# The transposed block's read, queued in front of a weight load instead of behind it

## The chip, the cores and the metric

The kernel runs on one core of a Trainium2 chip. The metric is device time in microseconds (us), median of three runs. One execution was also profiled: each instruction's start and duration, each DMA's issue and landing, and the clock granted to TensorE, which is full speed over the whole span.

## What the reference computes

A trunk of two layers over x of 256 positions by 2048 features. Each layer is a mixer (retention and a gated recurrence in layer 0, block attention in layer 1), an output projection, and then the part that matters here, a gated MLP with a causal convolution of width 3:

```python
def conv_ffn(h, w_up, conv_w, conv_b, w_down):
    u = causal_dwconv(h @ w_up, conv_w, conv_b)
    gate, val = jnp.split(u, 2, axis=-1)
    return (jax.nn.gelu(gate) * val) @ w_down
```

`w_up` is 2048 by 11264 (gate and value halves of 5632), `w_down` is 5632 by 2048, in float32.

## The kernel before

**Chunks and the ring.** All weights are streamed from DRAM in chunks of 256 rows by 512 columns (512 KB), 784 of them. A ring of four slots (`RING`) holds them. SyncE (SP) issues each load into `raw` (`load`, L322) once VectorE (DVE) has finished with the chunk four earlier in the same slot (`lo_ready`). ScalarE (ACT) rounds the chunk to `w_hi` (L498), DVE subtracts to get the rest, `w_lo` (L1147), and TensorE (PE) multiplies with both, 12 matmuls per chunk in up (L892 to L894). ACT may start a chunk only when it has landed and PE has used the chunk four earlier.

**A block of up.** Up has 22 blocks of 512 columns per layer: for each of 11 pairs a gate block (half 0) and a value block (half 1). A block is 8 chunks (c = 0 to 7). Pair 0 is written out, pairs 1 to 10 are a hardware loop over j, and down follows. PE writes a block with positions on the partitions, while the convolution wants features on them. So while the next block's chunks stream, the block is turned:

- after its `w_lo` of chunk 2, DVE transposes the block in 32 by 32 squares from PSUM to `cross` (L1310, L1311) and signals `acc_drained`;
- SP writes `cross` to the DRAM tensor `turn_line` with four DMAs of 128 KB (`put`, L342), behind the load of chunk 6 in its order;
- SP waits for the four to land (`put_out`), reads `turn_line` back to `h` with one DMA of 512 KB (`fetch`, L359), and signals `moved`;
- after `w_lo` of chunk 7, DVE scales `h` by the row norms (L1317), which waits for `moved`;
- ACT, after its `w_hi` of the following chunk 0, applies the first tap (L564, four instructions), which waits for L1317;
- DVE applies the two other taps after `w_lo` of chunks 1 and 2 (L1324, L1331), then transposes the next block, and so on.

Every engine goes through its instructions in program order; the order of SP is the order in which its transfers are queued. The loads that stand around a `fetch` are called A (chunk 7), B (chunk 0 of the next block) and C (chunk 1) below. ACT has a table load before `w_hi` of chunk 0 in every loop iteration (L498 ACT_TABLE_LOAD); so half of the Bs, those that open an iteration, have it behind them. A gate block is turned during the value block's chunks, so its `fetch` stands beside such a B; for a value block B is chunk 0 of half 1, and has no table load.

Of the kernel before, what the change touches and what calls it, by code (L numbers as in the profile page):

```python
# [130 lines left out]
def build(nc, x_t, params, w_gates, rope, decay, rel_bias, buckets, identity,  # L131
# [180 lines left out]
    @block.sync  # L312
    def _(sp):
        def load(w, q, c, cols, rows):

            s = c % RING
            turn = q + c // RING
            if not (isinstance(turn, int) and turn == 0):

                sp.wait_ge(lo_ready, RING * (turn - 1) + s + 1)  # L320
            src = w[bass.ds(rows * (CT * P), CT * P), cols].rearrange("(t p) n -> p t n", p=P)
            sp.dma_start(raw[:, s, :, :], src).then_inc(landed[s], 16)  # L322

        def put(n):

            sp.wait_ge(acc_drained, n + 1)
            write_quads()

        def put_x(k):

            sp.wait_ge(x_flipped, k + 1)
            write_quads()

        def put_qk(k):

            sp.wait_ge(qk_flipped, k + 1)
            write_quads()

        def write_quads():
            for i in range(QUADS):  # L340
                dst = turn_line[:, i, :].rearrange("(g c) n -> c g n", g=QUADS)
                sp.dma_start(dst, flip_quads[i * SQ:(i + 1) * SQ, :, :]).then_inc(put_out, 16)  # L342

        def put_probs(i):

            sp.wait_ge(probs_flipped, i + 1)
            for k in range(QUADS):
                dst = prob_line[:, k, :].rearrange("(g c) n -> c g n", g=QUADS)
                sp.dma_start(dst, probs_flip[k * SQ:(k + 1) * SQ, :, :]).then_inc(probs_out, 16)

        def fetch_probs(i):

            sp.wait_ge(probs_out, 16 * QUADS * (i + 1))
            sp.dma_start(probs_back[:, :, :], prob_line[:, :, :]).then_inc(probs_moved, 16)

        def fetch(k):

            sp.wait_ge(put_out, 16 * QUADS * (k + 1))
            sp.dma_start(h_quads[:, :, :], turn_line[:, :, :]).then_inc(moved, 16)  # L359

        for ph in phases:
            l = ph.layer
            for b, (_, _, col) in enumerate(ODD_BLOCKS if l else EVEN_BLOCKS):
                for c in range(KC):
                    if (l, b, c) == (0, 0, 0):
                        for u, landing in enumerate((tile_landed, landed[0])):
                            sp.dma_start(raw[:, 0, u, :], w_in[0][u * P:(u + 1) * P, col:col + NB]).then_inc(landing, 16)
                        continue
                    if (l, b, c) == (0, 0, 5):
                        sp.dma_start(par[:, 4 * KT:], params[:, 4 * KT:]).then_inc(const_loaded, 16)  # L370
                    load(w_in[l], ph.q_in + 2 * b, c, slice(col, col + NB), c)
                    if l and b >= 2 and b % 3 != 1 and b < 3 * MOVED_QK + 1:
                        k = 2 * ((b - 2) // 3) + (b % 3 == 0)
                        if c == 2:
                            put_qk(k)
                        if c == 4:
                            fetch(ph.m_in + k)
                    if l == 0 and b - 2 in MOVED_IN and c == 0:
                        fetch(MOVED_IN.index(b - 2))
                    if l == 0 and b - 1 in MOVED_IN and c == 6:  # L380
                        put(b - 1)
                    if l and b in (4, 7, 10) and c == 7:
                        put_probs(b // 3 - 1)
                    if l and b in (5, 8, 11) and c == 1:
                        fetch_probs(b // 3 - 1)
                    if (l, b, c) == (0, 0, 1):

                        sp.wait_ge(tile_landed, 16)
                    if (l, b) == (0, 0) and c in (1, 3, 4):
                        j = (1, 3, 4).index(c) + 1  # L390
                        part = slice(j * BT, (j + 1) * BT)
                        sp.dma_start(x_res[:, part, :], x_t[:, part, :]).then_inc(x_loaded[j], 16)
            for b in range(OUTB):
                for c in range(KC):
                    load(w_out[l], ph.q_out + 2 * b, c, slice(b * NB, (b + 1) * NB), MIX_ORDER[l][c])
                    if b >= 2 and c == 0:
                        fetch(ph.m_out + b - 2)
                    if b and c == 6:
                        put(ph.n_out + b - 1)
            for half in range(2):  # L400
                for c in range(KC):
                    load(w_up[l], ph.q_up + 2 * half, c, slice(half * D_FF, half * D_FF + NB), c)
                    if half == 0 and c == 0:
                        fetch(ph.m_up - 1)
                    if half and c == 6:
                        put(ph.n_up)
            with sp.Fori(1, PAIRS) as j:
                for half in range(2):
                    for c in range(KC):
                        load(w_up[l], ph.q_up + 4 * j + 2 * half, c, bass.ds(j * NB + half * D_FF, NB), c)  # L410
                        if c == 0:
                            fetch(ph.m_up + 2 * j + half - 2)
                        if c == 6:
                            put(ph.n_up + 2 * j + half - 1)
            for b in range(OUTB):
                cols = slice(b * NB, (b + 1) * NB)
                for c in range(FC) if b == 0 else DOWN_HEAD:
                    load(w_down[l], ph.q_down, FC * b + c, cols, c)
                    if b == 0 and c in (0, 8):
                        fetch(ph.m_down - 2 + c // 8)  # L420
                    if b == 0 and c == 6:
                        put(ph.n_down - 1)
                    if l and (b, c) == (0, 18):
                        put_x(0)
                    if l and (b, c) == (0, 20):
                        fetch(ph.m_down)
                    if l and b and c == 7:
                        put_x(b)
                    if l and b and c == 9:
                        fetch(ph.m_down + b)  # L430
                    if b and l == 0 and c == 6:
                        put(ph.n_down + b - 1)
                    if b and l == 0 and c == 8:
                        fetch(ph.m_down + b - 1)
                if b == 0:
                    continue
                with sp.Fori(*DOWN_TURNS) as t:
                    for i in range(RING):
                        load(w_down[l], ph.q_down + t, FC * b + i, cols, RING * t + i)
                for c in DOWN_TAIL:  # L440
                    load(w_down[l], ph.q_down, FC * b + c, cols, c)

        for t in range(2):

            sp.wait_ge(last_added, t + 1)
            sp.dma_start(out_t[:, t, (OUTB - 1) * NB:], x_nat[:, OUTB - 1, t, :]).then_inc(last_stored, 16)
        sp.wait_ge(last_stored, 16 * 2)
# [1367 lines left out]
```

## Time and profile before

| | us |
|---|---|
| median of three runs | 2202.23 |
| lowest, highest | 2201.97, 2204.25 |
| the profiled execution | 2206.41 |
| its span, first to last instruction | 2204.6 |
| PE busy, in the span | 2194.8 |
| DVE busy | 1514.0 |
| ACT busy | 1151.9 |
| share of the 16 DMA engines taken by SP's queue | 70.9% |

Up of layer 0 lies at about 360 to 870 us of the span, up of layer 1 at about 1460 to 1970. Ends of matmuls are modelled and overlap the next one's start, so gaps of PE are read from starts.

### The profile page before, as it was taken

What the parts mean: (1) busy time and instruction counts of PE and PEld (TensorE: products, weight loads), DVE (VectorE), ACT (ScalarE), POOL (GpSimd) and SP (SyncE); (2) the same over time, 40 slices, a digit from 0 to 9 for tenths busy, and PEclk for the clock granted to TensorE, in tenths of its full rate; (3) what the DMA queues carried; (4) which work ended last, traced back from release to release, by engine and by line L of the source; (5) the groups of instructions that cost most, each with busy time, mean ns of one, the idle gap of its engine ahead of it and who ended that gap; (6) DMA issues with size and microseconds to landing.
All of it is one profiled execution on the core that took longest, in us unless ns stands there. A gap on an engine that the chain in (4) does not pass through costs nothing.

```text
span 2204.6 us, 28872 instructions
## 1 busy us (share of the span) xinstructions
PE 2194.8 (100%) x10010; PEld 1827.4 (83%) x10010; DVE 1514.0 (69%) x1927; ACT 1151.9 (52%) x1440; POOL 7.7 (0%) x17
## 2 busy tenths in 40 slices
PE   9999999999999999999999999999999999999999
PEld 8888888888888888888888888888887888888887
DVE  7877766777777776655566576676777677766444
ACT  6554455555655655444455555555555556554443
POOL 0000000000000000000000000000000000000000
PEclk9999999999999999999999999999999999999999
DMA  8766667777787877766676786567777878777665
GB/s 272 216 214 202 203 207 224 224 236 242 236 250 233 249 229 248 222 203 206 205 232 216 223 265 200 182 217 239 231 238 227 249 234 248 230 248 240 216 214 162
DMA packets 267938, 497.97 MB, mean 226 GB/s; under 512 B 18790, under 2 KB 55670, under 8 KB 267729
## 3 DMA queue, kind: packets, MB, share of 16 engines
q1 hardware_dynamic: 265968, 490.68, 70.9%
q0 software_dynamic: 1456, 5.65, 0.7%
q8 instruction: 51, 0.84, 0.1%
q10 hardware_dynamic: 432, 0.56, 0.1%
q14 instruction: 31, 0.25, 0.0%
HBM read 456.16 MB, written 40.66 MB: 225 GB/s over the span
## 4 chain that ended last, share of the span: by engine, by line
PE 75%; DVE 8%; DMA 8%; issue 4%; ACT 3%; SPq 1%; DVEq 1%; ACTq 0%
PE ps L892 13%; PE ps L894 13%; PE ps L893 13%; PE ps L874 8%; PE ps L875 8%; PE ps L876 8%; DMA h<-turn_line 6%; PE ps L851 5%; PE ps L855 3%; ACT w_hi L498 1%; DMA turn_line<-cross 1%; DVE w_lo L1147 1%; DVE h L1317 1%; DVE pad_g L1331 1%; DVE pad_g L1324 1%
## 5 line engine op out<-in xcount | busy, mean ns | idle before, releaser
L1147 DVE TENSOR_TENSOR w_lo<-raw,w_hi 128x1024 fp32r<-128x1024 f32 x782 | 947.0, 1223 | 560.8 <-ACT w_hi L498 535.2
L498 ACT ACTIVATE w_hi<-raw 128x1024 fp32r<-128x1024 f32 x782 | 812.6, 1056 | 687.0 <-PE ps L876 256.3
L892 PE MATMUL ps<-w_hi,xs 128*128 128x512 f32 x2048 | 800.1, 391 | 2.1 <-DVE w_lo L1147 2.1
L893 PE MATMUL ps<-w_lo,xs 128*128 128x512 f32 x2048 | 797.6, 389 | 0.0
L894 PE MATMUL ps<-w_hi,xs 128*128 128x512 f32 x2048 | 797.6, 389 | 0.0
L892 PEld LDWEIGHTS ps<-w_hi,xs 128*128 128x128 f32 x2048 | 384.6, 188 | 84.0 <-DVE w_lo L1147 4.8
L894 PEld LDWEIGHTS ps<-w_hi,xs 128*128 128x128 f32 x2048 | 384.6, 188 | 80.1
L893 PEld LDWEIGHTS ps<-w_lo,xs 128*128 128x128 f32 x2048 | 384.6, 188 | 78.8
L874 PE MATMUL ps<-w_hi,act 128*128 128x512 f32 x808 | 315.0, 390 | 1.0 <-DVE w_lo L1147 1.0
L876 PE MATMUL ps<-w_hi,act 128*128 128x512 f32 x808 | 314.6, 389 | 0.0
L875 PE MATMUL ps<-w_lo,act 128*128 128x512 f32 x808 | 314.6, 389 | 0.0
L874 PEld LDWEIGHTS ps<-w_hi,act 128*128 128x128 f32 x808 | 151.7, 188 | 33.3 <-DVE w_lo L1147 1.4
L876 PEld LDWEIGHTS ps<-w_hi,act 128*128 128x128 f32 x808 | 151.7, 188 | 31.4
L875 PEld LDWEIGHTS ps<-w_lo,act 128*128 128x128 f32 x808 | 151.8, 188 | 31.2
L851 PE MATMUL ps<-act,w_hi 128*128 128x512 f32 (+1 forms) x304 | 95.5, 396 | 0.0
L1317 DVE TENSOR_TENSOR h<-h,rstd 128x1024 f32<-128x1024 f32 x44 | 53.9, 1226 | 43.6 <-DMA h<-turn_line 43.1
L851 PE MATMUL ps<-xs,w_hi 128*128 128x512 f32 x256 | 81.0, 398 | 2.0 <-DVE w_lo L1147 1.5
L855 PEld LDWEIGHTS ps<-act,w_lo 128*128 128x128 f32 x304 | 57.2, 188 | 13.4
L572 ACT ACTIVATE act<-pad_v 128x1024 f32 (+1 forms) x22 | 23.4, 1064 | 81.1 <-DVE pad_v L1341 81.1
L564 ACT ACTIVATE pad_v<-h,par 128x256 f32<-128x256 f32 x88 | 45.8, 592 | 34.4 <-DVE h L1317 34.4
L855 PE MATMUL ps<-act,w_lo 128*128 128x256 f32 (+1 forms) x304 | 59.8, 278 | 0.0
L855 PEld LDWEIGHTS ps<-xs,w_lo 128*128 128x128 f32 x256 | 48.1, 188 | 11.2
(209 smaller groups left out, 1132.6 us busy)
## 6 DMA issues: line engine op xcount, KB each, us to landing
raw<-w_up SPq DMA_DIRECT2D x352, 512.0 KB, 4.6
raw<-w_in SPq DMA_DIRECT2D x191, 512.0 KB, 4.4
raw<-w_down SPq DMA_DIRECT2D x176, 512.0 KB, 4.7
turn_line<-cross SPq DMA_DIRECT2D x276, 128.0 KB, 2.5
h<-turn_line SPq DMA_DIRECT2D x69, 512.0 KB, 6.0
raw<-w_out SPq DMA_DIRECT2D x64, 512.0 KB, 4.7
prob_line<-probs_t SPq DMA_DIRECT2D x12, 192.0 KB, 3.7
probs<-prob_line SPq DMA_DIRECT2D x3, 768.0 KB, 6.2
```

Of the source, the lines that this page charges most:

```text
L498: act_f(w_hi[:, s, :, :], raw[:, s, :, :], ACT.Copy).then_inc(hi_ready, 1)
L564: ins = act_f(by_quad(pad[:, t, 0:S]), h_tiles[:, :, t, :], ACT.Identity, scale=w, bias=b)
L851: return mm(ps[:, 4 * group + m, :], w_hi[:, s, u, m * P:(m + 1) * P], rhs, start=first and u == 0, stop=False)
L855: return mm(ps[:, 4 * group + m, 0:S], w_lo[:, s, u, m * P:(m + 1) * P], rhs[:, 0:S], start=False, stop=last and u == CT - 1)
L874: mm(out, x_hi, w_hi[:, s, u, :], start=first and u == 0, stop=False)
L875: mm(out, x_hi, w_lo[:, s, u, :], start=False, stop=False)
L876: ins = mm(out, x_lo, w_hi[:, s, u, :], start=False, stop=last and u == CT - 1)
L892: mm(out, x_hi, w_hi[:, s, u, :], start=first and u == 0, stop=False)
L893: mm(out, x_hi, w_lo[:, s, u, :], start=False, stop=False)
L894: ins = mm(out, x_lo, w_hi[:, s, u, :], start=False, stop=last and u == CT - 1)
L1147: tt(w_lo[:, s, :, :], raw[:, s, :, :], w_hi[:, s, :, :].bitcast(F32), ALU.subtract).then_inc(lo_ready, 1)
L1317: tt(h_tiles, h_tiles, scale, ALU.mult).then_inc(normed, 1)
```

## The change

In the whole of up, and in the first 9 chunks of down, `fetch` is issued one load earlier in SP's order: directly behind A instead of directly behind B. The number of transfers, their sizes, their targets and what each waits for stay the same. The read of the out projection's last block (`fetch(ph.m_up - 1)`) stays where it is.

```diff
                     if half and c == 6:
                         put(ph.n_up)
+                    if half and c == 7:
+                        fetch(ph.m_up)
             with sp.Fori(1, PAIRS) as j:
                 for half in range(2):
                     for c in range(KC):
                         load(w_up[l], ph.q_up + 4 * j + 2 * half, c, bass.ds(j * NB + half * D_FF, NB), c)
-                        if c == 0:
-                            fetch(ph.m_up + 2 * j + half - 2)
                         if c == 6:
                             put(ph.n_up + 2 * j + half - 1)
+                        if c == 7:
+                            fetch(ph.m_up + 2 * j + half - 1)
             for b in range(OUTB):
                 cols = slice(b * NB, (b + 1) * NB)
                 for c in range(FC) if b == 0 else DOWN_HEAD:
                     load(w_down[l], ph.q_down, FC * b + c, cols, c)
-                    if b == 0 and c in (0, 8):
-                        fetch(ph.m_down - 2 + c // 8)
+                    if b == 0 and c == 7:
+                        fetch(ph.m_down - 1)
```

## Rows read from the trace of the kernel before

**Rows 1.** Waits of PE over the whole span: total us, times, longest.
```profile
PE ps L892 <- DVE w_lo L1147: 2.1, 5, 0.9
PE ps L874 <- DVE w_lo L1147: 1.0, 1, 1.0
```

**Rows 2.** Timeline of PE at the last gap: start, us, [idle before <- releaser].
```profile
1968.51 0.39 PE L876 MATMUL ps<-w_hi,act 128*128 128x512 f32 x1
1969.91 0.50 PE L874 MATMUL ps<-w_hi,act 128*128 128x512 f32 x1 [1.01 <-DVE w_lo L1147]
```

**Rows 3.** Waits view of DVE for the read-back block, whole span.
```profile
DVE h L1317 <- DMA h<-turn_line: 43.1, 40, 2.9
```

**Rows 4.** Chain that ended last, layer 1: first and last L1317 of 21.
```profile
1515.57 1.24 DVE h L1317
...
1957.39 1.24 DVE h L1317
```

**Rows 5.** Timeline of SP, a gate block's turn: issues.
```profile
1814.03 1.79 SPq L342 DMA_DIRECT2D turn_line<-cross  x4
1818.02 0.40 SPq L322 DMA_DIRECT2D raw<-w_up  x1
1818.57 0.36 SPq L359 DMA_DIRECT2D h<-turn_line  x1
```

**Rows 6.** The same for the value block's turn just before it.
```profile
1792.47 1.79 SPq L342 DMA_DIRECT2D turn_line<-cross  x4
1795.20 0.40 SPq L322 DMA_DIRECT2D raw<-w_up  x1
1796.47 0.35 SPq L359 DMA_DIRECT2D h<-turn_line  x1
```

**Rows 7.** Waits of SP's queue for the four writes, whole span.
```profile
SPq L359 <- DMA turn_line<-cross: 47.5, 45, 2.9
```

**Rows 8.** Load B of rows 5, by its line: issue to landing.
```profile
DMA to landing us min/median/max: 5.0/5.0/5.0
```

**Rows 9.** Chain, pieces of the two reads: issue, us until landing.
```profile
1796.47 6.06 DMA h<-turn_line
...
1818.57 5.94 DMA h<-turn_line
```

**Rows 10.** Timeline of ACT behind the two Bs, value block first.
```profile
1801.39 1.06 ACT L498 ACTIVATE w_hi<-raw 128x1024 fp32r<-128x1024 f32 x1 [0.28 <-DMA raw<-w_up]
1803.96 2.08 ACT L564 ACTIVATE pad_v<-h,par 128x256 f32<-128x256 f32 x4 [1.51 <-DVE h L1317]
...
1823.08 1.28 ACT L498 ACT_TABLE_LOAD   x1 [2.05 <-DMA raw<-w_up]
1824.37 1.06 ACT L498 ACTIVATE w_hi<-raw 128x1024 fp32r<-128x1024 f32 x1
1826.01 2.08 ACT L564 ACTIVATE pad_g<-h,par 128x256 f32<-128x256 f32 x4 [0.57 <-DVE h L1317]
1828.00 3.02 ACT L498 ACTIVATE w_hi<-raw 128x1024 fp32r<-128x1024 f32 x3
```

**Rows 11.** Timeline of DVE: L1317 of three blocks (value, value, gate).
```profile
1715.78 1.23 DVE L1317 TENSOR_TENSOR h<-h,rstd 128x1024 f32<-128x1024 f32 x1 [1.56 <-DMA h<-turn_line]
...
1802.55 1.23 DVE L1317 TENSOR_TENSOR h<-h,rstd 128x1024 f32<-128x1024 f32 x1 [0.18 <-DMA h<-turn_line]
...
1824.53 1.23 DVE L1317 TENSOR_TENSOR h<-h,rstd 128x1024 f32<-128x1024 f32 x1 [1.03 <-DMA h<-turn_line]
```

**Rows 12.** Timeline of SP, the first read of layer 0 and load C.
```profile
415.01 0.35 SPq L359 DMA_DIRECT2D h<-turn_line  x1
415.65 0.39 SPq L322 DMA_DIRECT2D raw<-w_up  x1
```

**Rows 13.** Timeline of DVE, the first L1317 of layer 0.
```profile
419.76 1.23 DVE L1317 TENSOR_TENSOR h<-h,rstd 128x1024 f32<-128x1024 f32 x1 [0.60 <-DMA h<-turn_line]
```

**Rows 14.** Timeline of DVE and PE, fourth chunk of down in layer 0.
```profile
867.66 1.23 DVE L1147 TENSOR_TENSOR w_lo<-raw,w_hi 128x1024 fp32r<-128x1024 f32 x1
...
869.88 0.39 PE L874 MATMUL ps<-w_hi,act 128*128 128x512 f32 x1
```

## The prediction, made before the changed kernel was run

> **What bounds the kernel now.** I read the page first: PE is busy for nearly the whole span, at the full clock, so only its gaps can be won. The waits of PE [rows 1] hold little: 2.1 us over five waits and 1.0 us in one, all for `w_lo`. Read from starts (two matmuls of a run start 0.227 us apart), that last one is 1968.51 + 0.227 = 1968.74 wanted, 1969.91 got: 1.17 us [rows 2]. Four such gaps, all in or right behind layer 1's up, come to about 3.8 us with the slower matmul after each; layer 0's up has none. That is the most that the change can win.
>
> Next I asked what makes `w_lo` late: the chain that ended last. Through all of layer 1's up it holds no matmul. It goes round transposes, four writes, read back, L1317, L564, taps, next transposes. This round has its own pace: from the first to the last L1317 are 441.82 us over 20 blocks, 22.09 each [rows 4]. PE needs 8 chunks x 12 matmuls x 0.227 = 21.8. So in layer 1 the round is slower than PE and eats PE's reserve until PE waits; in layer 0 PE has a little reserve left at the end: `w_lo` of down's fourth chunk ends at 868.89, PE starts on it at 869.88, so (less 0.05 for the signal) 0.94 us [rows 14]. Each microsecond added to the round in a layer is paid beyond that reserve; PE's 100% hides this.
>
> The waits view gives the round's place for a gain: L1317 idles 43.1 us for the read in 40 cases [rows 3]. The question is whether an earlier read shortens the round, and the answer lies in who comes next: L564 stands on ACT behind `w_hi` of chunk 0, and that waits for B.
>
> **The change, part by part.** Nothing is added or removed; 44 reads change places with one load each.
>
> *The read's issue.* In value blocks the read already waits for the writes: they begin at 1792.47, it goes out at 1796.47, 4.0 us later, though B went at 1795.20 [rows 6]; 45 waits of SP, 47.5 us, are of this kind [rows 7]. In gate blocks B went 3.99 us after the writes' start and the read at 4.54 [rows 5]. So the read goes out about 0.5 us earlier in gate blocks, at no other time in value blocks. What it gains is the place in the queue.
>
> *The transfers.* In the gate block B lands at 1818.02 + 5.0 = 1823.0 [rows 5, 8], the read at 1818.57 + 5.94 = 1824.51 [rows 5, 9]. Both are 512 KB and SP's queue works in order there. I take it that they swap: the read lands near 1823.0 and B in the second place, near 1824.5. B's issue would be about 0.6 us behind the read (the distance from a read to the next load, 415.01 to 415.65 [rows 12]), at 4.0 + 0.6 = 4.6 after the writes' start, just where the read was. The pair starts a little sooner, so I take x = 0.1 us off B's new landing; bounds for x are -0.1 (no gain, B's smaller pieces last) and 0.5 (the whole 0.5 us of earlier issue). What is issued behind, C, keeps its place behind both.
>
> *Gate block, with table load.* Now: L1317 starts at 1824.53 and L564 1.48 later at 1826.01 [rows 10, 11]; `w_hi` was done at 1825.43, so L564 waits for L1317. After: L1317 runs early, 1.03 us of idle gone [rows 11], but B lands at 1824.41; then 0.08 to the table load, 1.28 of table load, 1.06 of `w_hi`, and L564 0.08 before its end (back-to-back ACT instructions overlap so: four taps end at 1828.09, the next starts at 1828.00 [rows 10]). That is 2.36 with rounding: L564 at 1826.77, 0.76 us LATER. Everything behind (second tap, third tap, transposes, next writes) follows L564 at a fixed distance (1803.96 to 1814.03, 10.07 us [rows 5, 10]). So a gate block costs +0.76, though its L1317 no longer waits.
>
> *The table load's price.* The row has it at 1.28 us, with `w_hi` 0.01 behind its end and no idle [rows 10]. The Trainium skill (ScalarE: Activation LUTs, What ACT_TABLE_LOAD costs) gives 1283 ns for the load and some 1380 ns for a drain, 2.66 us per switch. The load's figure agrees; the drain is not seen between landing and `w_hi`. By the page's whole price a gate block would cost 0.76 + 1.38 = 2.1 us instead of 0.76, and the change some 40 us; the measurement decides.
>
> *Value block, no table load.* B lands in the read's old place: 1796.47 + 6.06 - 0.1 = 1802.43 [rows 9]; plus 0.1 plus 1.06 less 0.08 gives 1803.51 for `w_hi`'s release of L564, before the 1803.96 of now. So here L1317 bounds, and its idle of 0.18 [rows 11] goes: a gain of 0.16. Where the idle is long (1.56 in the first row [rows 11]) `w_hi` bounds and the gain is 1.41 - 1.08 + 0.02 + 0.1 = 0.45. In layer 0 four of ten such blocks reach that cap, in layer 1 four, the rest gain 0.07 to 0.31; added up 2.5 us in layer 0 and 2.9 in layer 1. The gate block at the start of down has no table load: 0.45 more in each layer.
>
> *The first block of a layer.* Its read is issued at 415.01 and used at 419.76, 4.75 later [rows 12, 13], with both loads ahead already done, so moving it forward gains it nothing; B goes from before the writes' landing to 415.65 [rows 12] and lands behind the read. That costs 0.8 beyond the 0.76 (0.3 to 1.3).
>
> *Sum.* Ten gate blocks with a table load per layer. Layer 0: 10 x 0.76 + 0.8 - 2.5 - 0.45 = 5.45, less the reserve of 0.94: 4.5. Layer 1: 7.6 + 0.8 - 2.9 - 0.45 = 5.05, with no reserve (PE waits at the end already [rows 2]): 5.05. Together +9.6, on the profiled execution's 2206.41: 2216.0. The median of the runs is 4.2 lower; I carry the difference over: 2211.8, said as 2212.
>
> *Down* has a read in front of its ninth load instead of behind it; that is the last value block, counted above. Code, waits and queues elsewhere are untouched.
>
> **The rivals.**
>
> *B is not held (not slower).* The swap costs nothing if B, though queued second, lands by its own latency: 4.6 + 5.0 [rows 8] after the writes' start, 1823.6, L564 at 1825.96 against 1826.01. Gate blocks then cost nothing, value blocks gain, and all that is left is winning up to 3.8 us of PE's gaps: 2198.5 to 2203. For: the Trainium skill (DMA: Bandwidth & Descriptors, Queues, rings and completion order) says that completion is not FIFO per issuing engine, so an order of issue need not be one of landing. Against: B and the read, issued 0.55 apart, land 1.5 apart [rows 5, 8, 9], as transfers that queue for the same engines do. It decides from x = 0.9 on; between x = 0.5 and that, the gain of value blocks already cancels the gate blocks. No result over 0.2% faster fits, as the gaps hold only 0.17%; a small chance stays for a round that also stalls something I don't see.
>
> *The reserve takes it (same).* If the unprofiled runs have a faster round than this profile (they are 4.2 us shorter), each layer may have 2 to 3 us more reserve: 9.6 - 5 = +4.6, or less with x = 0.3: up to 2206.5.
>
> *SP stands longer (much slower).* SP now waits for the writes before B. If the writes land later with nothing queued between (they do by 2 us in a first block), then B, C and `w_hi` slip by more than I count. One more microsecond in each of ten gate blocks is 20 us: 2232. Against: the writes are ahead of all of this in the queue and landed at 4.0 in both kinds.
>
> **How the numbers follow.** My forecast, a gate block's cost of 0.5 to 1.0, has 0.68: its ends are x = 0.3 (some 3.5 us in all) and x = -0.1 (15 us), 2206 to 2217. B not held has 0.14, the reserve 0.10, SP longer 0.06, anything faster 0.02. For 8 in 10 I take the forecast's span, half of the reserve's case, and some of either side: 2203 to 2219. A run of this kernel tells about 0.2% (4.4 us) from no change. Slower by more: 0.63 of the forecast, 0.03 of the reserve, 0.06 of the last, and so 0.73 rounded; within: 0.23; faster: 0.04.
>
> **What the changed profile would show.** Step by step: the wait of L1317 for the read nearly gone (43 us to under 10); ACT's waits for `raw<-w_up` grown, the table load's above all; L564 of gate blocks waiting for nothing of DVE, about 0.76 us later after the writes' start than now (11.98 to 12.7), of value blocks 0.1 to 0.45 earlier; per pair the round slower by about 0.5; PE's waits for `w_lo` up from 3 to about 12 us, now in layer 0 too. The forecast is wrong if B lands less than 1 us after the read, or if the chain of layer 1 turns to matmuls.

## The result, and the profile of the changed kernel

| us | before | changed |
|---|---|---|
| median of six runs each | 2202.61 | 2215.62 |
| lowest to highest | 2200.47 to 2204.58 | 2212.64 to 2219.47 |
| span of the profiled execution | 2204.6 | 2217.6 |

The change makes the kernel 0.56% slower: ratio 1.0056, 95% interval 1.0047 to 1.0066. Medians and spans both differ by 13.0 us; both profiled executions lie about 4 us above the median of their kernel. Ratios and intervals here and below are taken over the single runs and are not quotients of the medians, from which they differ by up to 0.0006. All medians are over every run but one: a twelfth run of the kernel called hold below took 5745 us and is left out. In the changed file the lines are shifted: L1317 is now L1319, L564 is L566, L498 is L500, L1147 is L1149, L892 is L894; in the kernels of the experiments they are shifted by a few as well, and the text on them keeps the numbers of before.

First the waits of the changed kernel, those of PE and then those around the read (engine, what waited, for what: total us, times, longest):

```profile
PE ps L894 <- DVE w_lo L1149: 10.3, 18, 1.3
...
ACT w_hi L500 <- DMA raw<-w_up: 150.4, 61, 4.3
...
ACT L500 <- DMA raw<-w_up: 68.5, 20, 4.3
...
DVE h L1319 <- DMA h<-turn_line: 18.6, 23, 1.6
```

The wait for the read fell from 43.1 us [rows 3] to 18.6, as one would wish, but only in gate blocks: from the timelines of DVE, L1317's idle went from 31.7 to 2.2 us there and rose from 11.9 to 16.7 in value blocks. ACT's waits for loads of `w_up` rose instead: in the same view of before they were 77.8 us in front of `w_hi` and 41.0 us in the 20 cases where the table load comes first; now 150.4 and 68.5. PE's waits for `w_lo` went from 2.1 us [rows 1] to 10.3; 0.6 us of both stand in layer 1's input projection, the rest in up. From starts, PE's gaps of 0.08 us and more add up to 9.7 us in layer 0's up (0.1 before) and 6.5 in layer 1's with the first chunks of down (4.0 before): 12.2 of the 13.0. One of them in layer 0, where there were none (timeline of PE):

```profile
790.36 0.39 PE L896 MATMUL ps<-w_hi,xs 128*128 128x512 f32 x1
791.74 0.50 PE L894 MATMUL ps<-w_hi,xs 128*128 128x512 f32 x1 [0.99 <-DVE w_lo L1149]
```

A gate block of the changed kernel, in the timelines of SP, DVE and ACT:

```profile
722.68 1.79 SPq L342 DMA_DIRECT2D turn_line<-cross  x4
724.72 0.40 SPq L322 DMA_DIRECT2D raw<-w_up  x1
726.72 0.34 SPq L359 DMA_DIRECT2D h<-turn_line  x1
727.83 1.27 SPq L322 DMA_DIRECT2D raw<-w_up  x2
...
732.07 1.22 DVE L1319 TENSOR_TENSOR h<-h,rstd 128x1024 f32<-128x1024 f32 x1
...
733.23 1.28 ACT L500 ACT_TABLE_LOAD   x1 [3.48 <-DMA raw<-w_up]
734.52 1.06 ACT L500 ACTIVATE w_hi<-raw 128x1024 fp32r<-128x1024 f32 x1
735.49 2.07 ACT L566 ACTIVATE pad_g<-h,par 128x256 f32<-128x256 f32 x4
```

These answer to [rows 5] and the end of [rows 10, 11]. The read goes out 4.04 us after the first write, B at 5.15. L1319 starts with no idle, at 9.39. B lands at 10.45 (by its line: 5.3 us after its issue), then come table load, `w_hi`, and only then L566, at 12.81, although its input was ready at 732.07 + 1.22 = 733.29, 2.2 us earlier. Nothing idles between the table load and L566: the whole stretch hangs on B. The table load ends at 734.51 and `w_hi` starts at 734.52, so the drain of some 1380 ns that the Trainium skill (ScalarE: Activation LUTs, What ACT_TABLE_LOAD costs) adds to each switch is again not seen here.

The value block behind it, which answers to [rows 6]:

```profile
745.56 1.79 SPq L342 DMA_DIRECT2D turn_line<-cross  x4
...
749.53 0.34 SPq L359 DMA_DIRECT2D h<-turn_line  x1
750.15 1.64 SPq L322 DMA_DIRECT2D raw<-w_up  x3
...
754.77 1.23 DVE L1319 TENSOR_TENSOR h<-h,rstd 128x1024 f32<-128x1024 f32 x1 [0.79 <-DMA h<-turn_line]
...
756.15 1.06 ACT L500 ACTIVATE w_hi<-raw 128x1024 fp32r<-128x1024 f32 x1 [3.42 <-DMA raw<-w_up]
757.11 2.07 ACT L566 ACTIVATE pad_v<-h,par 128x256 f32<-128x256 f32 x4
```

The read still lands last for DVE, 9.2 us after the first write, with only A in front of it, and B lands at 10.5. ACT waits 3.42 us for B, and L566 follows at 11.55, back to back with `w_hi`. So it is everywhere: in the profile of before L564 starts behind L1317 in all 44 blocks of up, in the changed one back to back with `w_hi` in all 44.

In layer 1 the chain that ended last now goes through the load where the read was [rows 9]:

```profile
1607.89 2.48 DMA turn_line<-cross
1610.39 0.34 SPq L359
...
1611.27 5.83 DMA raw<-w_up
1617.21 0.10 ACT L500
...
1619.96 1.15 ACT pad_g L566 x3
...
1630.87 2.57 DMA turn_line<-cross
1633.45 0.34 SPq L359
1634.07 5.95 DMA raw<-w_up
...
1894.61 1.24 DVE w_lo L1149
1895.89 0.50 PE ps L894
```

It does so in 13 of the 17 blocks up to 1895.9 us; four gate blocks it passes by L1319. From the last two lines on, to the end of up, it runs along matmuls: PE's last gap of this layer is the one just before 1895.89.

### The profile page after: what moved, and what is told of

Same layout as the page of the kernel before. It is cut to its first block, busy times and chain, and to the rows that moved or that the text cites. A ratio compares the mean times of both kernels' runs of the same rounds, so it can differ in the third digit from the quotient of the medians.

```text
span 2217.6 us, 28872 instructions
## 1 busy us (share of the span) xinstructions
PE 2199.6 (99%) x10010; PEld 1825.0 (82%) x10010; DVE 1511.1 (68%) x1927; ACT 1140.7 (51%) x1440; POOL 7.7 (0%) x17
## 4 chain that ended last, share of the span: by engine, by line
PE 60%; DMA 12%; DVE 10%; issue 8%; ACT 6%; SPq 2%; DVEq 1%; ACTq 1%
PE ps L894 8%; PE ps L896 8%; PE ps L895 8%; PE ps L878 8%; PE ps L876 8%; PE ps L877 8%; DMA raw<-w_up 8%; PE ps L853 5%; DMA turn_line<-cross 3%; PE ps L857 3%; ACT w_hi L500 3%; SPq L342 2%; ACT pad_g L566 1%; DVE pad_g L1333 1%; DVE pad_g L1326 1%
## 5 line engine op out<-in xcount | busy, mean ns | idle before, releaser
L1149 DVE TENSOR_TENSOR w_lo<-raw,w_hi 128x1024 fp32r<-128x1024 f32 x782 | 945.5, 1222 | 601.8 <-ACT w_hi L500 588.0
L500 ACT ACTIVATE w_hi<-raw 128x1024 fp32r<-128x1024 f32 x782 | 806.2, 1054 | 682.0 <-PE ps L878 238.8
L894 PE MATMUL ps<-w_hi,xs 128*128 128x512 f32 x2048 | 802.2, 392 | 10.7 <-DVE w_lo L1149 10.3
L894 PEld LDWEIGHTS ps<-w_hi,xs 128*128 128x128 f32 x2048 | 384.5, 188 | 100.2 <-DVE w_lo L1149 21.1
L857 PEld LDWEIGHTS ps<-act,w_lo 128*128 128x128 f32 x304 | 57.1, 188 | 13.4
L1319 DVE TENSOR_TENSOR h<-h,rstd 128x1024 f32<-128x1024 f32 x44 | 53.8, 1223 | 18.9 <-DMA h<-turn_line 18.6
L500 ACT ACT_TABLE_LOAD x20 | 25.7, 1283 | 68.5 <-DMA raw<-w_up 68.5
L857 PEld LDWEIGHTS ps<-xs,w_lo 128*128 128x128 f32 x256 | 48.1, 188 | 11.3
```

Source lines behind the costliest of these rows:

```text
L500: act_f(w_hi[:, s, :, :], raw[:, s, :, :], ACT.Copy).then_inc(hi_ready, 1)
L857: return mm(ps[:, 4 * group + m, 0:S], w_lo[:, s, u, m * P:(m + 1) * P], rhs[:, 0:S], start=False, stop=last and u == CT - 1)
L894: mm(out, x_hi, w_hi[:, s, u, :], start=first and u == 0, stop=False)
L1149: tt(w_lo[:, s, :, :], raw[:, s, :, :], w_hi[:, s, :, :].bitcast(F32), ALU.subtract).then_inc(lo_ready, 1)
L1319: tt(h_tiles, h_tiles, scale, ALU.mult).then_inc(normed, 1)
```

## The experiments

Two theories. **Q, landing of B:** L564 starts at the later of L1317's end and the end of `w_hi` of chunk 0; the change takes the first off the round and makes the second later, because B lands behind the read. **S, SP stands:** what costs is that SP waits for the writes and so issues B late. S puts most of the loss into value blocks, where B's issue moved by 1.9 us; Q puts it into gate blocks, where the table load lies behind B.

The landings, issues and taps of this table are us after the block's first write, means over the blocks of one profiled execution (18 gate blocks without the first and last of a layer, 20 value blocks), worked out from the timelines and landings; "tap" is the start of L564, layer 0 / layer 1. "gaps" are PE's gaps of 0.08 us or more in up of layer 0 / 1 and the first chunks of down behind it, added up. "median" is that of the runs.

| | gate: read out, lands | B out, lands | tap | value: read out, lands | B out, lands | tap | gaps | median |
|---|---|---|---|---|---|---|---|---|
| before | 4.6, 10.8 | 4.0, 9.5 | 12.11 / 12.55 | 4.0, 9.9 | 2.8, 8.2 | 11.25 / 11.39 | 0.1 / 4.0 | 2203.2 |
| changed | 4.0, 8.9 | 5.0, 10.4 | 12.81 / 12.72 | 4.0, 9.1 | 4.6, 10.5 | 11.67 / 11.52 | 9.7 / 6.5 | 2215.6 |
| gate_only | 4.0, 8.8 | 5.0, 10.3 | 12.58 / 12.70 | 4.0, 9.9 | 2.8, 8.2 | 11.41 / 11.30 | 6.4 / 4.7 | 2212.3 |
| value_only | 4.6, 10.5 | 4.0, 9.2 | 11.85 / 12.14 | 4.0, 9.1 | 4.6, 10.5 | 11.57 / 11.61 | 0.1 / 1.7 | 2204.2 |
| after_warm | 4.0, 8.8 | 5.0, 10.3 | 11.49 / 11.37 | 4.0, 9.2 | 4.6, 10.6 | 11.76 / 11.72 | 0.5 / 0.1 | 2202.3 |
| before_warm | 4.6, 10.7 | 4.0, 9.3 | 12.18 / 12.27 | 4.0, 10.0 | 2.8, 8.4 | 11.36 / 11.44 | 0.7 / 2.1 | 2204.2 |
| gate_warm | 4.0, 8.7 | 5.0, 10.4 | 11.64 / 11.73 | 4.0, 9.9 | 2.7, 8.3 | 11.53 / 11.47 | 0.1 / 0.1 | 2201.2 |
| hold | 4.7, 10.2 | 4.3, 8.9 | 11.61 / 11.76 | 4.7, 10.4 | 4.2, 9.1 | 11.68 / 11.89 | 0.1 / 2.8 | 2208.0 |
| behind_c | 6.6, 12.9 | 4.0, 8.6 | 14.29 / 14.46 | 4.3, 11.3 | 2.8, 8.3 | 12.84 / 12.54 | 34.3 / 33.9 | 2272.5 |
| pool_read | 4.3, 10.3 | 4.0, 10.7 | 12.99 / 13.11 | 4.3, 11.4 | 2.8, 8.4 | 12.74 / 12.93 | 21.2 / 24.2 | 2249.1 |

"before" in the last column is from the runs beside the first four experiments (27 runs); beside the last four it was 2203.4 (23 runs). But for its median each row is one execution, and two executions of one order differ: before and before_warm, which both have L564 behind L1317, lie up to 0.3 us apart in the mean tap of a layer.

### Gate blocks alone

```diff
+                        if half and c == 0:
+                            fetch(ph.m_up + 2 * j + half - 2)
                         if c == 6:
                             put(ph.n_up + 2 * j + half - 1)
-                        if c == 7:
+                        if half and c == 7:
                             fetch(ph.m_up + 2 * j + half - 1)
```

This is against the changed kernel; in down the read of the last value block goes back to c == 8.

> The read goes ahead of load B for gate blocks alone (22 of 44); value blocks keep the order of before. Theory Q (B lands behind the read, the table load and w_hi of chunk 0 follow, and L564 waits for them): in the profile of the full change L564 of gate blocks came 0.70 us later in layer 0 and 0.17 in layer 1 (means of 9), and 1.3 to 1.8 in each first block; so 9 x 0.70 + 1.8 less the reserve of 0.9, plus 9 x 0.17 + 1.3, less some 0.5 each for the block at down's start: 6 to 10 us over before, 2209 to 2212. Theory S (what costs is that SP stands for the writes and issues B late): B is issued only 0.9 to 1.1 us later here against 1.9 in value blocks, so a third of the 13 us: 2206 to 2207.

Measured 2212.34, ratio 1.0038 (1.0024 to 1.0052): +9 us, within Q's 6 to 10 over the kernel before and far over S's 2206 to 2207. The tap of gate blocks moved nearly as with the full change (12.58 and 12.70 against 12.81 and 12.72). Set against the changed kernel, the value blocks' share is the remaining 3.3 us.

### Value blocks alone

```diff
-                        if c == 0:
+                        if half == 0 and c == 0:
                             fetch(ph.m_up + 2 * j + half - 2)
                         if c == 6:
                             put(ph.n_up + 2 * j + half - 1)
+                        if half == 0 and c == 7:
+                            fetch(ph.m_up + 2 * j + half - 1)
```

Against the kernel before; in down the last read moves from c == 8 to c == 7.

> The read goes ahead of B for value blocks alone, those without a table load behind B. Theory Q: L564 of these came 0.42 us later in layer 0 and 0.13 in layer 1 (means of 10 blocks with the full change); 4.2 less the reserve of 0.9, plus 1.3: +3 to +6 us, 2205.5 to 2208.5. Theory S: two thirds of the 13 us, 2211. The prediction's own step (value blocks gain 0.25 each) would give 2199 to 2202.

Measured 2204.24, ratio 1.0006 (0.9997 to 1.0015). B goes out 1.8 us later in these blocks and the time hardly moves: S falls. Q's +3 to +6 was too much as well, and the gain that the prediction had counted did not come: the tap is 0.3 and 0.2 us later, not 0.25 earlier. That loss does not show in the time, and the reserve of 0.9 us alone would not cover ten times 0.3. In this execution the gate blocks' taps came 0.3 and 0.4 earlier than in the profile of before, so that a pair took no longer; whether that is the scatter of executions or follows from the change isn't shown.

### The table load taken off B

```diff
     qk_small, _ = place("qk_small", [P, 4, 8])
+    warm, _ = place("warm", [P, 8])
...
             with eng.Fori(1, PAIRS) as j:
+                act_f(warm[:, 0:1], ones[:, 0:1], ACT.Gelu_apprx_tanh)
                 for c in range(KC):
                     split(ph.q_up + 4 * j, c)
```

This is ACT's loop. The tiny Gelu waits for nothing, so the iteration's table load comes in front of it, while ACT would idle for B. It loads the set that the pair's Gelu needs, so the second table load of the pair falls away too. It was added to the changed kernel and, as a control, to the kernel before.

> The full change, and ahead of each loop iteration one tiny Gelu on ScalarE that waits for nothing, so that the table load no longer stands between B's landing and w_hi of chunk 0. Theory Q: L564 of gate blocks then comes 1.28 us sooner than with the change, at about 11.5 us after the writes' start against 12.1 to 12.5 before; value blocks keep +0.42 and +0.13. Over a pair the round is then shorter than before by 0.2 to 1.0 us, PE's gaps in up go: 2198 to 2202, at or under before. Theory S: SP's order is untouched, so it stays at 2213 to 2217. A theory that the landing of the read itself sets the round would also say 2213 to 2217.

Measured 2202.30, ratio 0.9994 (0.9985 to 1.0003), 0.3 us over Q's range and at the level of before: the 13 us are gone, with SP's order untouched. The tap of gate blocks came from 12.81 and 12.72 to 11.49 and 11.37, by 1.32 and 1.35, the table load's 1.28. PE's gaps in up are down to 0.5 and 0.1 us.

> The kernel before with the same tiny Gelu alone; a control. Theory Q: in the order of before L564 of gate blocks waits for L1317 (norm) and not for w_hi, which is done 0.1 us earlier; without the table load w_hi has 1.3 us to spare and nothing moves: 2200 to 2203.5. If the table load by itself costs time elsewhere on the round, it comes out at 2198 to 2199, the floor that PE's gaps of 3.8 us leave.

Measured 2204.16, ratio 1.0000 (0.9991 to 1.0009), 0.7 us over Q's range but no change against the kernel before. Without the change the same Gelu is worth nothing, since L564 waits for L1317 there. So the table load costs nothing in one order of two transfers and some 13 us in the other. The missing second table load brings nothing in the order of before, and in the changed order the tap moved by the length of one load; so it is not what helped.

### Both together

Gate reads ahead of B, value reads behind it, and the tiny Gelu.

> Reads ahead of B for gate blocks alone, with the tiny Gelu that takes the table load off B; value blocks as before. Theory Q adds up: L564 of gate blocks at 11.4 to 11.5 us after the writes' start (12.1 and 12.5 before), of value blocks at 11.3 to 11.4 as before; a pair of 42.9 us is under PE's 43.5, PE's gaps in up vanish. 2200 to 2203: with PE bound everywhere it can't come out under the full change with the Gelu (2202.3) by more than 1 us.

Measured 2201.23 (2200.78 to 2202.25, 11 runs), ratio 0.9993 (0.9985 to 1.0002). The timeline of ACT at an iteration's start:

```profile
720.65 1.28 ACT L809 ACT_TABLE_LOAD   x1
721.95 0.20 ACT L809 ACTIVATE warm<-ones 128x1 f32<-128x1 f32 x1
722.35 1.06 ACT L503 ACTIVATE w_hi<-raw 128x1024 fp32r<-128x1024 f32 x1 [0.20 <-PE ps L900]
723.31 2.06 ACT L569 ACTIVATE pad_g<-h,par 128x256 f32<-128x256 f32 x4
725.28 1.04 ACT L503 ACTIVATE w_hi<-raw 128x1024 fp32r<-128x1024 f32 x1
727.74 1.06 ACT L503 ACTIVATE w_hi<-raw 128x1024 fp32r<-128x1024 f32 x1 [1.42 <-PE ps L900]
```

The table load is out of the way before B lands. The view names PE as what released `w_hi` in this block, but by the landings `w_hi` starts 0.11 us behind B's, the distance that it has in 14 of the 20 blocks whose B opens an iteration; in the other 6 PE holds it longer. The taps are early enough (11.64 and 11.73) that PE no longer waits for `w_lo` in up; these are the longest waits that the view of PE's holds, the third of them in layer 1's input projection:

```profile
PE ps L1048 <- POOL ones L457: 1.0, 1, 1.0
...
PE ps L857 <- DVE xs L1216: 0.6, 1, 0.6
...
PE ps L898 <- DVE w_lo L1153: 0.6, 2, 0.3
```

It is the fastest of the kernels, but the interval holds no change. What it does show is the spread: 1.5 us over 11 runs, where the kernel before had 6.7 over 23 on the same chip (standard deviations 0.5 and 2.0). The likely reason is that with PE setting the pace the chance in the transfers' landings no longer reaches the time; no run separates this from other reasons.

### SP held, the order kept

```diff
+                        if c == 0:
+                            sp.wait_ge(put_out, 16 * QUADS * (ph.m_up + 2 * j + half - 1))
                         load(w_up[l], ph.q_up + 4 * j + 2 * half, c, bass.ds(j * NB + half * D_FF, NB), c)
```

> The order of before (read behind B), but SP waits for the four writes before it issues B, so B goes out as late as with the change in value blocks (4.0 us instead of 2.7), and the read right behind it (4.6 instead of 4.0). Theory Q, L564 = the later of L1317 and w_hi: in value blocks the read lands some 0.7 us later and L1317 with it, gate blocks don't change (B goes at 4.0 there anyway): 10 x 0.7 less 0.9, plus 10 x 0.7: 2212 to 2218. If only B's own lateness counts for nothing and the read's 0.6 us neither, as moving value blocks alone (2204.2) may suggest, 2203 to 2205.

Measured 2207.97 (11 runs), ratio 1.0017 (1.0008 to 1.0026), between the two expectations. With B out 1.5 us later and the read 0.7, the read lands only 0.5 later in value blocks: B had not been all that held it. In gate blocks it landed 0.6 earlier than in the profile of before, for which I have no cause beyond the scatter of executions. So the sum came out wrong, though L564 followed L1317 in every mean (the read's landing plus 1.41 gives 10.35 + 1.41 = 11.76 in value blocks, measured 11.68 and 11.89). The profiled execution took 2205.0 us, 2.9 under the median of its kernel, so its means don't account for the whole 4.6 us.

### One place further back

```diff
-                        if c == 0:
+                        if c == 1:
                             fetch(ph.m_up + 2 * j + half - 2)
```

Against the kernel before; in down the last two reads move from behind c == 0 and 8 to behind 1 and 9.

> The read one place further back than before, behind load C. Theory Q: B lands as before, the read one transfer (1.3 us) later in value blocks and 1.3 to 1.9 in gate blocks, L1317 and L564 with it, in all 44 blocks: 2245 to 2275. So the order of before would stand between two slower ones. If the read's landing had 1 us or more to spare, under 2215.

Measured 2272.46, ratio 1.0315 (1.0300 to 1.0330), as Q had it. DVE's waits for the read:

```profile
DVE h L1317 <- DMA h<-turn_line: 116.1, 44, 4.3
```

All 44 blocks wait, 116 us against 43 [rows 3], and 2.1 us of later landing in gate blocks and 1.4 in value blocks are 3.4 us for a pair, some 70 in the two layers; the time grew by 69 and PE's gaps by 64. So the place of before lies between two that are slower.

### The read on another queue

This is against the kernel before. SP issues no read of `turn_line` in up beyond the out projection's, and none of up's two in down. GpSimd does, on its own queue and with a semaphore of its own; here for layer 0:

```diff
+        for k in range(phases[0].m_up, phases[0].m_down):
+            pool.wait_ge(put_out, 16 * QUADS * (k + 1))
+            pool.dma_start(h_quads[:, :, :], turn_line[:, :, :]).then_inc(moved_up, 16)
```

> SP issues no read in up and doesn't wait for the writes; GpSimd issues each read on its own queue when they have landed, at 4.0 us, and B keeps its own time of issue (2.7 and 4.0). Theory Q says that B's place decides: B is in front as before and the read's landing is what counts. If the two queues share the engines packet by packet, B lands 0.3 to 0.7 us later and the read earlier in gate blocks; if GpSimd's issue costs 1 us more, the read lands at 10 to 11. 2200 to 2212; not near the change's 2215 unless B lands after 10 us.

Measured 2249.09, ratio 1.0213 (1.0200 to 1.0226), far outside. In gate blocks B, issued at 4.0 as before and in front of the read, now lands at 10.7 instead of 9.5; in value blocks B is spared and the read lands at 11.4 instead of 9.9. The taps follow: in gate blocks `w_hi` sets them (it ends at 13.1 and 13.2), in value blocks L1317, 1.5 us later than before. So B didn't have to stand behind the read in a queue to be late; it is enough that both are under way. The Trainium skill (DMA: Bandwidth & Descriptors, Rules for kernel authors) says that the queues of SP, ACT and GpSimd run on the same 16 DMA engines and interleave, so that spreading gives no bandwidth; this run agrees, with B landing 1.2 us later for a read on another queue. PE's waits:

```profile
PE ps L898 <- DVE w_lo L1153: 34.3, 39, 1.4
```

## Why the prediction was right, and where its sizes were off

**The round sets the loss: right.** Its pace, not PE's busy share, decided. Each tap's shift, added up, gives PE's gaps: in layer 0, 9 x 0.70 for gate blocks, 1.70 for the first (12.29 to 13.99), 10 x 0.42 for value blocks, 1.70 back for the block at down's start (13.51 to 11.81), less the reserve of 0.94: 9.6, and the gaps grew by 9.6. In layer 1: 9 x 0.17 + 1.12 + 10 x 0.13 - 1.10 = 2.85; the gaps grew by 2.6. From a tap to the next block's first write it is 10.04 to 10.07 us in the mean of either kind, before and changed, so a tap's shift is the round's.

**Gate blocks: the mechanism was right, the size right in one layer.** Expected +0.76, measured +0.70 in layer 0 and +0.17 in layer 1. B's new landing against the read's old one, x, was taken as 0.1; it was 0.2 in layer 0, and 0.7 in layer 1, where the reads of before had been slow (11.05 on average) and the new loads were not (10.35). Part of that 0.17 is one slow execution: value_only and before_warm, which have L564 behind L1317 too, put layer 1's gate taps at 12.14 and 12.27 instead of 12.55. Over the three such kernels against the two with the read ahead and the table load in place, a gate block costs 0.65 and 0.39. B's landing was forecast right (1824.41 is 10.4 after the first write; measured 10.45 and 10.35), its issue was not: 1.1 and 0.9 us behind the read instead of 0.6, at 5.1 and 4.9 instead of 4.6.

**Value blocks: the term that failed.** The step was "value block, no table load: B lands in the read's old place", a gain of 0.25 in the mean. Measured is a loss of 0.42 and 0.13. The read did not move up by a whole transfer: with only A in front of it, it took 5.0 to 5.2 us and landed at 9.1, 0.6 to 0.8 before its old time and not 1.6 (its old distance to B). It could go out no earlier, and its own time from issue to landing was the bound; in the order of before B's transfer ran within that time. B then follows 1.4 us behind it, at 10.5 instead of 9.9. In x this is -0.5 to -0.8, outside my bounds of -0.1 to 0.5. Nor did L1317's idle go: A landed 0.9 earlier too, DVE was ready 0.9 earlier, and the idle in front of L1317 rose from 0.6 to 0.8. Over the four kernels with the read behind B in value blocks and the three with it ahead, the loss is 0.28 and 0.22 a block. The first block's term had just this mechanism (expected 0.76 + 0.8, measured 1.70 and 1.12); I had not carried it to the value blocks, where the writes' landing binds the read's issue in the same way.

**The block at down's start** was put at 0.45 gained and gained 1.70 and 1.10: its reads of before were among the slowest (2.77 and 2.64 us of idle in front of L1317).

So the sum of +9.6 against +13.0 came out near for partly wrong reasons, and that is luck: value blocks gained 2.5 and 2.9 us in my sum and lost 4.2 and 1.3 in the trace, and layer 1's gate blocks were far cheaper, so that errors of both signs cancelled in part. Of the signs that the prediction named, L1317's wait did not fall under 10 us (18.6, all but 2.2 of it in value blocks), the taps of gate blocks came at 12.8 and 12.7 (named: 12.7), and PE's waits rose to 10.3 us, layer 0 included. A pair's round grew by 1.1 and 0.3 us (named: about 0.5). Of the two signs of being wrong, B landing less than 1 us behind the read stayed away (1.8 and 1.3 us in gate blocks, 1.4 and 1.3 in value blocks), and the other came for a part: for the last 79 us of layer 1's up the chain is matmuls. The round was the slower of the two only up to there; the taps of the four blocks behind it came at 11.6, 11.7, 11.2 and 12.3 us (before 11.4, 12.5, 11.5 and 13.4), and PE had no further gap.

**The rivals.** B not held: it lands 1.3 to 1.9 us behind the read, in the means of every kernel that has it there, so held it is, though the other queue's run shows that the order in one queue is not the only way to hold it. The reserve was no larger than read: medians and profiles both grew by 13.0. SP standing longer fell with the value blocks alone.

## What to carry to other kernels

When a wait in a trace is to be shortened by moving its transfer up, look at what the consumer's consumer waits for next: here the read fed a DVE step with slack to gain, but ACT had to get past the displaced load first, with a table load behind it. A transfer put in front of another gains less than the other loses when its own time from issue to landing is the bound: in value blocks the read gained 0.8 us and B lost 2.3. And work that costs nothing in an idle stretch (a table load, 1.28 us) becomes a cost when the next thing on the path starts to wait behind it; issuing it early takes it off again.

## What I had not expected of the hardware

Load A of value blocks lands 6.8 to 7.2 us after the first write in the six kernels that issue B 0.7 us behind it, and at 5.9 to 6.1 in the four that issue B 2 us or more behind it (changed, value_only, after_warm, hold; means by layer, landings of the trace). A was issued at the same 2.0 to 2.2 us in all of them, and is in front of B. A load close behind thus goes with a landing 0.9 us later, in the mean, of one that was queued before it. It is not so in every block: A lands after 6.6 us in 80 of 120 blocks of the six kernels, and in 4 of 80 of the four. And a read on GpSimd's queue slows a load of SP's that was issued before it by 1.2 us. What in the engines does this was not tried.
